# Row projections of both attention blocks: pieces among the last attention units, and the order of weight splits behind them

## What is computed

```python
# first block
a   = dilated_attention(q, k, v, rel_bias)        # 4 merged heads x 128
y_a = a @ w_attn_out                             # 512 -> 1024
y_c = silu(layer_norm(conv(glu))) @ conv_pw_w    # 1024 -> 1024
out = (g_a * y_a + g_c * y_c) @ w_out            # 1024 -> 1024
x   = x + rms_norm(out);  x = x + rms_norm(ffn(x))
# second block
x   = x + 0.5 * swiglu(x)
y_a = rwkv7_mixer(...) @ rwkv_proj               # 512 -> 1024
y_b = forgetting_attention(...) @ fox_proj       # 512 -> 1024
x   = x + (gate_a * y_a + gate_b * y_b) @ w_out_2
x   = x + 0.5 * swiglu(x)
```

## Time and profile before

| | |
|---|---|
| median of the timed runs | 1188.65 us (1188.22 to 1189.52) |
| the profiled execution | 1190.72 us, span 1188.6 us |
| TensorE matmuls busy | 1141.8 us, 96% of the span |
| VectorE, ScalarE, GpSimd busy | 766.1 us, 559.8 us, 157.8 us |
| mean granted clock of TensorE | 0.984 |
| HBM read | 186.74 MB, 159 GB/s over the span |
| first block's row chunks and w_out | 245.8 to 307 us |
| second block's attention units | 880 to 948 us |
| second block's fox_proj and w_out_2 | 948 to 989 us |

### The profile page before, as it was taken

The page is one execution under the profiler, slowest core; times in us unless marked ns, Lnnn a source line. Parts: engine busy times, 40 slices in busy tenths (PEclk is TensorE's granted clock), DMA queues, the critical chain, the costliest instruction groups (busy, mean ns, idle before and its releaser), DMA issues.

```text
span 1188.6 us, 22077 instructions
## 1 busy us (share of the span) xinstructions
PE 1141.8 (96%) x9584; PEld 1076.7 (91%) x9584; DVE 766.1 (64%) x1034; ACT 559.8 (47%) x669; POOL 157.8 (13%) x113
## 2 busy tenths in 40 slices
PE   7999999989899999899999999999999889999997
PEld 7999999988799999799999988999888778999996
DVE  4888976746687686864555567864267555645564
ACT  6333445483665454563444368322334536444343
POOL 5888760000000000000000001032000000000000
PEclk9999999999999999999999998999999899999999
DMA  8586553344366655635655544323024333565651
GB/s 257 181 288 206 178 166 118 118 160 150 107 206 199 205 179 177 209 110 192 198 186 167 190 152 154 107 78 104 19 90 142 128 106 121 194 214 177 209 161 54
DMA packets 144314, 188.93 MB, mean 159 GB/s; under 512 B 4448, under 2 KB 128921, under 8 KB 144237
## 3 DMA queue, kind: packets, MB, share of 16 engines
q1 hardware_dynamic: 142941, 184.28, 47.4%
q0 software_dynamic: 1104, 3.49, 0.8%
q10 hardware_dynamic: 192, 0.05, 0.0%
HBM read 186.74 MB, written 2.64 MB: 159 GB/s over the span
## 4 chain that ended last, share of the span: by engine, by line
PE 86%; DVE 7%; ACT 4%; issue 2%; DMA 0%; ACTq 0%; DVEq 0%
PE bank L2004 20%; PE bank L2006 20%; PE bank L2005 20%; PE bank L2118 6%; PE bank L2119 6%; PE bank L2120 5%; PE bank L556 2%; DVE w_lo L1619 2%; ACT w_hi L1334 2%; PE bank L624 1%; PE bank L2245 1%; DVE bank L1836 1%; PE bank L2063 1%; DVE x L1693 1%; PE bank L531 1%
## 5 line engine op out<-in xcount | busy, mean ns | idle before, releaser
L2004 PE MATMUL bank<-X_hi,w_hi 128*128 128x256 f32 x1840 | 526.5, 286 | 3.3 <-issue 2.6
L2006 PE MATMUL bank<-X_hi,w_lo 128*128 128x256 f32 x1840 | 522.8, 284 | 0.0
L2005 PE MATMUL bank<-X_lo,w_hi 128*128 128x256 f32 x1840 | 522.7, 284 | 0.0
L1334 ACT ACTIVATE w_hi<-w_raw 128x2048 fp32r<-128x2048 f32 x171 | 326.2, 1909 | 177.6 <-PE bank L2006 133.1
L1619 DVE TENSOR_TENSOR w_lo<-w_raw,w_hi 128x2048 fp32r<-128x2048 f32 x146 | 334.1, 2289 | 78.0 <-ACT w_hi L1334 77.7
L2004 PEld LDWEIGHTS bank<-X_hi,w_hi 128*128 128x128 f32 x1840 | 355.0, 193 | 8.3 <-issue 6.3
L2005 PEld LDWEIGHTS bank<-X_lo,w_hi 128*128 128x128 f32 x1840 | 355.1, 193 | 1.2
L2006 PEld LDWEIGHTS bank<-X_hi,w_lo 128*128 128x128 f32 x1840 | 354.9, 193 | 0.0
L1731 DVE TENSOR_TENSOR arena<-bank,rstd 128x512 f32<-128x512 f32 x66 | 45.6, 691 | 184.8 <-PE bank L2006 179.6
L1282 POOL TENSOR_TENSOR w_lo<-w_raw,w_hi 128x2048 fp32r<-128x2048 f32 x24 | 111.2, 4644 | 32.2 <-ACT w_hi L1334 32.0
L2118 PE MATMUL bank<-w_hi,Y_hi 128*128 128x512 f32 x264 | 103.3, 391 | 1.2 <-DVE Y_lo L1759 1.2
(11 more groups left out here) (285 smaller groups left out, 1307.1 us busy)
## 6 DMA issues: line engine op xcount, KB each, us to landing
w_raw<-in_ffn_w_dram SPq DMA_DIRECT2D x66, 1024.0 KB, 5.4
w_raw<-in_w_in_dram SPq DMA_DIRECT2D x53, 1024.0 KB, 5.2
w_raw<-in_w_up_dram SPq DMA_DIRECT2D x22, 1024.0 KB, 5.1
w_raw<-in_w_down_dram SPq DMA_DIRECT2D x11, 1024.0 KB, 4.9
w_raw<-in_w_out_dram SPq DMA_DIRECT2D x8, 1024.0 KB, 4.9
w_raw<-in_conv_pw_w_dram SPq DMA_DIRECT2D x4, 1024.0 KB, 4.9
w_raw<-in_w_attn_out_dram SPq DMA_DIRECT2D x2, 1024.0 KB, 5.1
w_raw<-in_rwkv_proj_dram SPq DMA_DIRECT2D x2, 1024.0 KB, 5.1
```

Source lines behind the costliest of these rows:

```text
L1334: a.activation(w_hi[slot][:, :], raw[slot][:, :], ACT.Copy).then_inc(S["w_hi"], told.one("w_hi"))
L2004: pe.matmul(o, wh, xh, start=start, stop=False, skip_group_check=True)
L2005: pe.matmul(o, wh, xl, start=False, stop=False, skip_group_check=True)
L2006: return pe.matmul(o, wl, xh, start=False, stop=stop, skip_group_check=True)
```

## The change

In the second block RP0 and RP1 are cut. RP0's first k-tile stays ahead of unit 5 and starts with six tiles in bank 3 and the two gate banks that are free first; the last two tiles go to the bank of the last gate chunk. RP0's second k-tile stands ahead of unit 6. RP1 is cut in four: three tiles behind unit 6's turning, five tiles ahead of unit 7, three tiles behind unit 7's turning, five tiles behind unit 7. FP1 goes by pairs and tells VectorE of each. ScalarE and VectorE split FP1 in unit 6 (and nothing in units 5 and 7), WO0 behind the first gates' work and WO1 behind the first two pairs of the gated sum. In both blocks VectorE gates, adds and subtracts in the order: gate, add, gate of the next pair, low part of the first, add, low part. In the first block VectorE's split of chunk A_WO + 1 moves from ahead of the gating to behind the first two pairs.

```diff
+            last_gate = bank_of[B_GA + 7]
+            free_first = [3] + [b for b in range(3) if b != last_gate] + [last_gate]
+
+            def rwkv_rows(r, k, o0, o1):
+
+
+                tiles = [2 * b + m for b in free_first for m in range(2)]
+                if r == 0 and k == 0 and o0 == 0:
+                    for b in free_first[1:3]:
+                        pe.wait_ge(S[f"bank{b}_read"], all_read(B_RP)[b])
+                by_rows(B_RP + r, (B_RP + r) % RING, 0, Y_hi, Y_lo, 2 * r, r == 0, r == 1,
+                        part=[(k, o) for o in tiles[o0:o1]], ends=k == 1 and o1 == NT)
...
                 if it < 5:
                     columns(B_GA + 3 + it, midway=(lambda: f_scores(1)) if it == 0 else None)
-                elif it < 7:
-
-                    r = it - 5
+                if it == 5:
                     pe.wait_ge(S["y_lo"], 1)
+                    rwkv_rows(0, 0, 0, 6)
                     for b, c in enumerate(all_read(B_RP)):
                         pe.wait_ge(S[f"bank{b}_read"], c)
-                    by_rows(B_RP + r, (B_RP + r) % RING, 0, Y_hi, Y_lo, 2 * r, r == 0, r == 1)
+                    rwkv_rows(0, 0, 6, NT)
+                if it == 6:
+                    rwkv_rows(0, 1, 0, NT)
+                if it == 7:
+                    rwkv_rows(1, 0, 3, NT)
...
                 if it + 2 < FUNITS:
                     f_scores(it + 2)
+                elif it == 6:
+                    rwkv_rows(1, 0, 0, 3)
+                else:
+                    rwkv_rows(1, 1, 0, 3)
...
+            rwkv_rows(1, 1, 3, NT)
...
-                    by_rows(n, n % RING, 4, Y_hi, Y_lo, HT + 2 * r, r == 0, r == 1)
+                    by_rows(n, n % RING, 4, Y_hi, Y_lo, HT + 2 * r, r == 0, r == 1, final=r == 1)
...
                 if it + 2 < FUNITS:
                     f_exps(it + 2)
+                if it == 6:
+                    split(B_FP + 1)
                 act.wait_ge(S["f_pv_done"], it + 1)
                 a.activation(Y_hi[:, HT + t, i * P:(i + 1) * P], bank[7][:, 0:P], ACT.Copy).then_inc(
                     S["f_out_hi"], told.one("f_out_hi"))
-                if it < 7:
+                if it < 5:
                     split(B_GA + 3 + it + 3)
...
-                if n > B_FP:
+                if n >= B_WO:
                     split(n + 2)
                 if n == B_FP:
...
                         a.activation(flat(g), flat(g), ACT.Sigmoid).then_inc(S["gate_2"], told.one("gate_2"))
+                        if lo == 0:
+                            split(B_FP + 2)
                 for p in ((0, 1) if n == B_WO - 1 else (2, 3) if n == B_WO else ()):
                     act.wait_ge(S["mixed"], 4 + p + 1)
                     a.activation(X_hi[:, 2 * p:2 * p + 2, :], gate_2a[:, 2 * p:2 * p + 2, :], ACT.Copy).then_inc(
                         S["mixed_hi"], told.one("mixed_hi"))
+                if n == B_FP + 1:
+                    split(n + 2)
...
-                if it < 7:
+                if it < 5:
                     split(n + 3)
+                if it == 6:
+                    split(B_FP + 1)
...
-                if n > B_FP:
+                if n >= B_WO:
                     split(n + 2)
                 if n == B_FP:
                     dve.wait_ge(S["gate_2"], 1)
...
-                ps = (0, 1) if n == B_WO - 1 else (2, 3) if n == B_WO else ()
-                for p in ps:
+                    split(B_FP + 2)
+
+                def gated(p):
+                    if p < 3:
+                        dve.wait_ge(S["pair_summed"], 3 + p + 1)
+                    else:
+                        dve.wait_ge(S["chunk_used"], B_WO)
                     dve.wait_ge(S["gate_2"], 2)
-                    dve.wait_ge(S["chunk_used"], B_WO)
-                    ga, gb = gate_2a[:, 2 * p:2 * p + 2, :], gate_2b[:, 2 * p:2 * p + 2, :]
+                    gb = gate_2b[:, 2 * p:2 * p + 2, :]
                     v.tensor_tensor(gb, gb, pairs(4 + p), ALU.mult).then_inc(S["dve_step"], told.one("dve_step"))
                     dve.wait_ge(S["dve_step"], told.value("dve_step"))
+
+                def mixed(p):
+                    ga, gb = gate_2a[:, 2 * p:2 * p + 2, :], gate_2b[:, 2 * p:2 * p + 2, :]
                     v.tensor_tensor(ga, ga, gb, ALU.add).then_inc(S["mixed"], told.one("mixed"))
-                for p in ps:
-                    ga = gate_2a[:, 2 * p:2 * p + 2, :]
+
+                def mixed_low(p):
                     dve.wait_ge(S["mixed_hi"], 4 + p + 1)
-                    v.tensor_tensor(X_lo[:, 2 * p:2 * p + 2, :], ga, X_hi[:, 2 * p:2 * p + 2, :].bitcast(F32),
-                                    ALU.subtract).then_inc(S["mixed_lo"], told.one("mixed_lo"))
+                    v.tensor_tensor(X_lo[:, 2 * p:2 * p + 2, :], gate_2a[:, 2 * p:2 * p + 2, :],
+                                    X_hi[:, 2 * p:2 * p + 2, :].bitcast(F32), ALU.subtract).then_inc(
+                        S["mixed_lo"], told.one("mixed_lo"))
+
+                if n == B_WO - 1 or n == B_WO:
+                    p = 0 if n < B_WO else 2
+                    gated(p)
+                    mixed(p)
+                    gated(p + 1)
+                    mixed_low(p)
+                    mixed(p + 1)
+                    mixed_low(p + 1)
+                if n == B_FP + 1:
+                    split(n + 2)
 
         block = ctx.enter_context(nc.Block())
 
@@ -1927,7 +1975,7 @@
...
-                if n < A_WO - 1:
+                if n < A_WO - 2:
                     split(n + 3)
                 if n == A_PA:
                     silu_low(2)
...
                 if n == A_WO - 1 or n == A_WO:
+                    p = 0 if n < A_WO else 2
+                    gated(p)
+                    mixed(p)
+                    gated(p + 1)
+                    mixed_low(p)
+                    mixed(p + 1)
+                    mixed_low(p + 1)
+                if n == A_WO - 1:
+                    split(A_WO + 1)
                 if A_WO - 1 <= n < A_END - 1:
                     split(n + 3)
...
-            def by_rows(n, slot, first_bank, hi, lo, k0, first, last, final=False):
-
-
-                split_ready(n)
-                steps = [(k, o) for k in range(2) for o in range(NT)]
+            def by_rows(n, slot, first_bank, hi, lo, k0, first, last, final=False, part=None, ends=True):
+
+
+                steps = part or [(k, o) for k in range(2) for o in range(NT)]
+                if part is None or part[0][0] == 0:
+                    split_ready(n)
...
-                mm.then_inc(S["chunk_used"], told.one("chunk_used"))
+                if ends:
+                    mm.then_inc(S["chunk_used"], told.one("chunk_used"))
```

## The result

| | before | after |
|---|---|---|
| median of the timed runs beside each other | 1189.09 us (1188.22 to 1190.97) | 1175.53 us (1174.74 to 1175.89) |
| the profiled execution | 1190.72 us, span 1188.6 | 1174.74 us, span 1172.9 |
| mean granted clock in it | 0.984 | 0.989 |

The ratio is 0.9886 (95% interval 0.9872 to 0.99): 13.6 us faster. Predicted were 17.9 us and 1170.8 us; the measured median lies 4.7 us above that and just above the range's upper end of 1175.5.

What follows compares the result with a forecast made beforehand. TensorE, busy 96% of the span, bounds it. Second block 8.21 waits + 6.19 half clock - 0.5 new waits = 13.9; first block 2.31 + 1.71 = 4.0; 1188.65 - 17.9 = 1170.75, say 1170.8 us; range 1168.0 to 1175.5.

Steps and rivals of the forecast that it cites:

- Waits: TensorE's waits go: 8.21 us around units 5 to 7 and second projection, 2.31 in first block; new waits cost 0.5.
- First block: Ahead of w_out: the 2.31 us wait goes, with 1.71 of half clock; gain 4.0 us, or 2.3 if half clock stays.
- Second block: Units 5 to 7 and projections: waits 8.21, half clock 6.19, new waits -0.5; gain 13.9 us.
- Rivals 1 to 4: Half clock stays (0.2); VectorE and ScalarE set the pace (0.12); weights' chain makes it slower (0.01); part not won (0.06).
- VectorE and ScalarE never set the pace: Rival claim: at five places with 1.1 to 1.3 us spare, their chain runs late; about 4 us, 1174.8; chance 0.12.
- no bank was late: Rival claim: a wait stays behind a bank taken as free; 1.7 to 2.6 us, 1173.4; chance 0.06.
- no weight came late: Rival claim: w_out's four chunks and FP1 each come a landing late; 24.5 us, 1195.3; chance of slower 0.01.
- rival 1: Second block: half clock stays, as work comes in 1 to 3 us pieces; 1.7 us a stretch, 1172.5 to 1175.9; chance 0.2.
- half-clock term: Half-clock stretches beside the removed waits go: 6.19 us in the second block, 1.71 in the first.
- likeliest case: Whole kernel: the forecast of 1169.0 to 1172.5 us, its two ends by moved half-clock stretches elsewhere; chance 0.55.
- rival 5: Elsewhere in the kernel: half-clock stretches move, one more or less, 1.7 us; 1169.1 or 1172.5; no separate chance given.

Runs made afterwards that it cites:

- filled kernels: Dummy matmuls put into TensorE's waits: kernel before with four unchanged-stage fills and its own waits filled, mean 1180.84 us; changed kernel with the four unchanged-stage fills, 1169.86 us.
- s13 to s16: Beside each other on one chip: changed kernel unaltered 1174.57 us, changed with four fills 1169.85, kernel before with four fills 1187.45, before with all fills 1180.86.
- all fills: Kernel before with the four fills plus dummy matmuls in its own waits of 2.31, 0.85, 1.78, 1.38 and 3.50 us: mean 1180.84 us.
- four fills: Dummy matmuls in unchanged stages (waits of 3.64 and 1.95 us, two hand-overs), cut to length: kernel before mean 1186.69 us, changed kernel 1169.86 us.

## Why the prediction was wrong

Right, step by step:
- **Waits.** 8.21 + 2.31 less 0.5 new is 10.0; the traces have 10.3, with one new wait of 0.18 instead of 0.2 and 0.3. Between the filled kernels it is 11.0, and A and B of their profiles give the same (64.71 - 62.15 = 2.6, 104.19 - 95.79 = 8.4), with what the dummies in before's own waits cost.
- **First block.** 4.27 against 4.0 where the stretch was there; 66.24 - 63.64 = 2.6 where it was not, which the prediction gave as 2.3.
- **Second block.** 13.92 against 13.9; B of before is 111.2 in both profiles of it, so between these profiles the price of the half clock held. From the end of unit 4 to w_out_2's fourth chunk, 967.83 - 923.1 = 44.7, as said.
- **Rivals 1 to 4.** No half clock stayed: 921 to 966 is at 1.00 in the first profile, and B is 97.3 in all five unfilled profiles with this edit, so VectorE and ScalarE never set the pace, no bank was late and no weight came late. Pieces of 1 to 3 us among small matmuls kept 1.00. The swinging between two clocks that the Trainium skill, "TensorE: Matmul & The Clock Gate", section "A second HAM failure mode: psum-queue depth-cycling", tells of was not seen in these stages. The argument against rival 1 was better than the prediction put it: of the 1716 matmuls of 780 to 850, 144 are of a dense step, in eight groups of about 1 to 3 us, so just such pieces held 1.00 there.

Wrong: **the half-clock term of the sum, 6.19 + 1.71 = 7.9 us, with nothing set against it outside the two stages.** The sum took every half-clock stretch of one profiled execution as a fixed price of its wait ("a wait is thus paid twice here"), and the unchanged stages as equal. In the mean of executions all half clock together was worth 3.9 us (14.2 less the 10.3 of waits), or 4.2 (+-0.9) by the granted clock. Two parts of the shortfall can be told apart with the fills, as far as their condition holds:
- in place 5.9 to 6.5 (+-0.9) and not 7.9. The wait of 2.31 was followed by half clock in five profiles of seven that have it, the 3.50 by none, one or two stretches. With the waits the change is worth 16.8 (+-1.2) in place; 17.9 is at the very end of that, and on the one chip where all these kernels ran beside each other it is 17.6 (1187.45 - 1169.85). So this part is small and barely clear of noise.
- outside, 2.6 (+-1.3) given back where the likeliest case had nothing and rival 5 at most 1.7 either way, with no reason for a sign. This is the larger part.

16.8 less 2.6 is 14.2 by construction and no check of the two. The profiled pair has other parts: 18.2 won in place and 2.5 given back, 15.7 in the span and 16.0 in time (1190.72 - 1174.74); that the median fell by 13.6 only is where the two executions stood, 1.6 us above the median beside it (1189.09) and 0.8 below (1175.53). That its 18.2 lies so close to the 17.9 is in part luck: the forecast was made from one of these two executions, and with the second profile of before, which lacks the stretch behind the 2.31, it is 16.5. The step that let this through is the one from 1190.72 to the median. The profiled execution had a clock of 0.984 and gave up 18.7 us to half clock, where the mean of 89 executions is 0.9867 and 15.8: a sign that stretches come and go, and I carried the sum over unchanged. The range, at 1.7 us for one stretch, was too narrow: over 93 executions the kernel before alone spreads by 6.7 us. The Trainium skill, same page, section "What's actually happening", says that the number of slow matmuls at a kernel's start differs between runs of the same kernel. The traces agree (a stretch that begins between 11 and 13 us is there in seven of the ten unfilled profiles). They show such a difference between runs in mid-kernel too.

**Open.** Why the unchanged stages lose more in after, and how firm the 2.6 us are. "Always at the hand-over" is refuted. The profiles lean that way weakly: with after's first block there are two, two, none, one and none stretches between 303 and 314 (the fifth is the first block's edit alone), with before's none, one, one, one and none. On the one chip where the four kernels ran beside each other (s13 to s16) the difference is 2.8 (1174.57 - 1169.85 less 1189.38 - 1187.45), but +-2.0 with so few executions. Whether another change that arrives earlier would lose as much was not tried.

## What to carry to other kernels

Waits can be forecast from one trace to tenths of a microsecond: here they repeat. Half clock can't: compare the mean granted clock of many executions with that of the profiled one before its stretches are priced, give each stretch a chance, and let one or two stretches in untouched stages come or go. More profiles alone would not have been enough here, as both of before have four stretches in B. Where a wait of 0.7 to 3.6 us can't be removed, matmuls of no use in a free bank keep the clock; here they brought 4.6 us in six such waits when cut a little shorter than the wait, and 1.5 us when too long.

## What was not expected of the hardware

- Half clock came without any wait too. In all 18 profiles one to three stretches stand between 722 and 735, in a stage where TensorE is busy without a gap. It works there in part on matmuls that use 32 or 64 of the 128 partitions. After, stretch and rows:

```profile
720.00:740.00 20.00, 20.00 (x117) 16.57 (x117) 13.13 (x20) 16.21 (x22) 4.33 (x1) 0.83 0.48 156
```

```profile
724.82 0.70 PE L494 MATMUL bank<-arena 64*128 64x256 f32 x2
725.44 0.69 PE L495 MATMUL bank<-arena 32*128 32x256 f32 x2
726.07 1.17 PE L494 MATMUL bank<-arena 64*128 64x256 f32 x2
```

  The use of few partitions isn't enough for it: in 780 to 850 of before, at 1.00, most matmuls use 64, as this group does. What makes the clock fall at 722 was not tried.

```profile
L556 PE MATMUL bank<-arena 64*64 64x64 f32 x896 | 27.9, 219 | 0.0
```

- With all fills the kernel before repeats far better: 1180.32 to 1182.11 us over 11 executions, with a standard deviation of 0.5 us, where without it was 1186.03 to 1192.68 over 93, with 1.4. The four fills alone don't do that: 2.1 us in before, and 1.3 in the changed kernel, which has 1.1 without.
- A plain fp32 matmul of 128 by 128 columns is two records and takes 0.22 us.
